# The last two experts' outputs added by one-hot products in PSUM

## What is computed

```python
combine = jnp.sum(jax.nn.one_hot(expert_id, N_EXPERTS) * (g_w[:, None] * top_w)[..., None], axis=1)
def expert_step(acc, inp):
    wg, wu, wd, c = inp
    hid = jax.nn.silu(t @ wg) * (t @ wu)
    return acc + c[:, None] * (hid @ wd), None
y, _ = lax.scan(expert_step, jnp.zeros_like(t), (w_gate, w_up, w_down, combine.T))
x = x + y
return rmsnorm(x, final_norm_w)
```

## Time and profile before

| | |
|---|---|
| time before, median of 3 runs | 468.01 us (467.56 to 470.87) |
| span of the profiled execution | 468.6 us, 7159 instructions |
| PE, PEld, DVE busy | 447.5, 387.4, 343.1 us (96%, 83%, 73%) |
| ACT, POOL busy | 275.6, 159.2 us (59%, 34%) |
| DMA | 94.57 MB, mean 202 GB/s |
| chain that ended last | PE 60%, DVE 20%, DMA 9%, ACT 6% |

### The profile page before, as it was taken

The page is one execution under the profiler, slowest core; times in us unless marked ns, Lnnn a source line. Parts: engine busy times, 40 slices in busy tenths (PEclk is TensorE's granted clock), DMA queues, the critical chain, the costliest instruction groups (busy, mean ns, idle before and its releaser), DMA issues.

```text
span 468.6 us, 7159 instructions
## 1 busy us (share of the span) xinstructions
PE 447.5 (96%) x2769; PEld 387.4 (83%) x2769; DVE 343.1 (73%) x527; ACT 275.6 (59%) x462; POOL 159.2 (34%) x120
## 2 busy tenths in 40 slices
PE   8999999999999899999999998999999999999873
PEld 7678887899997798999999988888888888888641
DVE  4456999756768889899775358677887788777835
ACT  6753555235562162338253335689999999979525
POOL 4660000000004001113300404288878887885210
PEclk9999999999999999999999998999999999999979
DMA  8850223240202033143299512989999999998256
GB/s 306 342 234 25 88 90 111 78 166 8 91 0 92 15 121 121 61 147 124 84 374 306 234 39 61 321 306 368 380 374 350 374 376 380 364 328 326 95 180 237
DMA packets 21200, 94.57 MB, mean 202 GB/s; under 512 B 4860, under 2 KB 7080, under 8 KB 12840
## 3 DMA queue, kind: packets, MB, share of 16 engines
q1 hardware_dynamic: 14424, 83.53, 47.7%
q0 software_dynamic: 4096, 8.41, 5.5%
q10 hardware_dynamic: 2640, 2.11, 1.4%
HBM read 88.79 MB, written 11.54 MB: 214 GB/s over the span
## 4 chain that ended last, share of the span: by engine, by line
PE 60%; DVE 20%; DMA 9%; ACT 6%; issue 3%; SPq 0%; DVEq 0%; POOLq 0%; ACTq 0%
PE bank L1695 32%; DMA raw<-in_w_gate_up_dram 5%; PE bank L2031 5%; PE bank L2033 5%; PE bank L2032 4%; DVE arena L1186 3%; PE bank L2019 2%; PE bank L1771 2%; DVE wl L1107 2%; PE bank L1896 2%; DMA arena<-pairs_dram 1%; ACT wh L765 1%; DMA pairs_dram<-arena 1%; DVE actl L1566 1%; DMA X<-h_dram,arena 1%
## 5 line engine op out<-in xcount | busy, mean ns | idle before, releaser
L1695 PE MATMUL bank<-wh,acth 128*128 128x256 f32 x320 | 91.9, 287 | 0.8 <-DVE actl L1101 0.8
L1695 PE MATMUL bank<-wh,actl 128*128 128x256 f32 x320 | 90.6, 283 | 0.0
L1695 PE MATMUL bank<-wl,acth 128*128 128x256 f32 x320 | 90.6, 283 | 0.0
L1695 PEld LDWEIGHTS bank<-wh,acth 128*128 128x128 f32 x320 | 61.3, 192 | 1.1 <-issue 1.0
L630 POOL TENSOR_TENSOR wl<-raw,wh 128x2048 fp32r<-128x2048 f32 x4 | 20.2, 5038 | 122.0 <-ACT wh L765 122.0
L1695 PEld LDWEIGHTS bank<-wl,acth 128*128 128x128 f32 x320 | 61.3, 192 | 0.0
L1695 PEld LDWEIGHTS bank<-wh,actl 128*128 128x128 f32 x320 | 61.3, 191 | 0.0
L709 POOL TENSOR_TENSOR wl<-raw,wh 128x1024 fp32r<-128x1024 f32 x15 | 36.0, 2417 | 42.7 <-ACT wh L960 42.7
L2031 PE MATMUL bank<-wh,acth 128*128 128x512 f32 x124 | 50.0, 403 | 0.1
L2033 PE MATMUL bank<-wh,actl 128*128 128x512 f32 x124 | 48.7, 393 | 0.0
L2032 PE MATMUL bank<-wl,acth 128*128 128x512 f32 x124 | 48.4, 390 | 0.0
(11 more groups left out here) (378 smaller groups left out, 1038.6 us busy)
## 6 DMA issues: line engine op xcount, KB each, us to landing
arena<-in_w_gate_up_dram SPq DMA_DIRECT2D x18, 1024.0 KB, 15.1
raw<-in_w_units_dram SPq DMA_DIRECT2D x17, 1024.0 KB, 4.9
arena<-in_w_down_dram SPq DMA_DIRECT2D x16, 1024.0 KB, 13.2
raw<-in_w_gate_up_dram SPq DMA_DIRECT2D x14, 1024.0 KB, 15.6
arena<-pairs_dram SPq DMA_DIRECT2D x6, 512.0 KB, 7.2
arena<-in_x_first_dram SPq DMA_DIRECT2D x3, 768.0 KB, 7.8
arena<-in_x_dram SPq DMA_DIRECT2D x4, 512.0 KB, 12.5
arena<-in_x_dram SPq DMA_DIRECT2D x1, 2048.0 KB, 11.0
```

The costliest lines, as they stand in the source:

```text
L1695: ins = te.matmul(acc_ap, a, b, start=(j == 0), stop=(j == n - 1))
```

## The change

A new list LAST names the last two experts in the order, 14 and 15. Their outputs are no longer scattered to memory and loaded back.

- Early in the run, SP copies x to the 512 late rows of pairs_dram (memory to memory), so that rows which no expert has written hold finite values; POOL and DVE wait for that copy (xrows_in).
- gates moves from the end of the loop to just behind expert 1 on DVE, with four more small instructions there, and four (slot_rows) that bring the token number of each slot of experts 14 and 15 into a tile. SP stores the late gates to gates_dram at expert 8, POOL gathers them by slot with two small indirect DMAs at expert 12 (slot_gates), and sets two small tiles to zero earlier.
- For experts 14 and 15, DVE writes chosen[j], a 112 x 512 one-hot from slot to token (choose). PE writes their down products to banks 2, 3 and 7, 4, without waiting for the copies of the expert before. ACT's copy into ysb multiplies by the gate of the slot.
- SP loads the late rows when experts 0 to 13 are scattered, not 0 to 15. Early tiles 0 and 1 get their gate and residual on POOL (multiplication of tile 0, both additions) and ACT (multiplication of tile 1, behind a wait for all four early loads, in ACT's program of expert 14, ahead of the copy of expert 15's hidden activation; the square root table is loaded there too). Tiles 2 and 3 stay on DVE.
- DVE writes late * r1[19] + early into PSUM, two halves of 128x512 for each of the 4 tiles (base_ok). The factor r1[19] is the late gate, or 0 where the token's late expert is 14 or 15. PE then adds two products per half, chosen[j] with ysb, onto it: 16 f32 products of 128x512. All four tiles are squared by ACT and scaled by DVE out of PSUM, as tiles 2 and 3 were.
- The products L2120, L2123 and L2128 go. The branch to later rounds stands at the end of every engine's program (all_rounds; for SP ahead of the stores), with a second set of sums inside it.

```diff
-        late_diag = [gate[:, 0, i * P:(i + 1) * P] for i in range(2)]
+        LAST = (NE - 2, NE - 1)
+        chosen = [raw[:, 0, j * T:(j + 1) * T] for j in range(2)]
+        slot_gate = [part(4) for _ in LAST]
+        slot_row = part(2 * TT).rearrange("p (j t) -> p j t", j=2)
...
-        def later_rounds(eng, body):
+        last_cols = slice(PERM[LAST[0]], PERM[LAST[1]] + 1, PERM[LAST[1]] - PERM[LAST[0]])
+        out_banks = {LAST[0]: (2, 3), LAST[1]: (7, 4)}
+        sum_banks = ((0, 1), (5, 6), (2, 3), (7, 4))
+        FIN = TT + 1
+
+        def down_banks(e, first_round):
+            return out_banks.get(e, (5, 6)) if first_round else (5, 6)
+
+        def all_rounds(eng, body, before=None, after=None):
 
             eng.wait_ge(routed, 1)
             n = eng.value_load(rounds[0:1, 0:1], min_val=1, max_val=MOST)
             with eng.If(n > 1):
-                with eng.Fori(1, n) as r:
+                eng.wait_ge(fin_ok, FIN)
+                if before is not None:
+                    before()
+                with eng.Fori(1, n + 1) as r:
                     body(r, r * NE)
-            return n
+                if after is not None:
+                    after(n)
 
...
+                if u == U["i"][0]:
+                    sp.dma_start(pairs_dram[T:2 * T, :], x[0]).then_inc(xrows_in, 16)
             sp.wait_ge(hg_ev, TT)
-            sp.dma_start(xres, x[0].rearrange("(t p) n -> p t n", p=P)).then_inc(xres_in, 16)
+            sp.dma_start(xres, x[0].rearrange("(t p) n -> p t n", p=P)).then_inc(xrows_in, 16)
...
-                        if e == 0:
-                            sp.wait_ge(early_ok, r * TT)
-                        else:
-                            sp.wait_ge(wlb_ok, (base + max(e - WSETS + 1, 0)) * 2)
+                        sp.wait_ge(wlb_ok, (base + max(e - WSETS + 1, 0)) * 2)
                         load_b(e)
-
-            def load_early(rows_done, first_round=False):
+                    if first_round and e == NE // 2:
+                        sp.wait_ge(gates_ok, 1)
+                        sp.dma_start(gates_dram.rearrange("(t p) n -> p t n", p=P), rs).then_inc(small_dma, 16)
+
+            def scattered(rows_done):
                 for j in range(YB):
                     sp.wait_ge(sca_out[j], rows_done)
-                if first_round:
-                    wait_a(sp, 0, NE - 2)
-                    sp.wait_ge(wlb_ok, (NE - 2) * 2)
+
+            def load_early():
                 for tt in range(TT):
                     sp.dma_start(early[tt], pairs_dram[tt * P:(tt + 1) * P, :]).then_inc(early_in, 16)
 
-            def sp_later(r, base):
-                sp_round(r, base)
-                load_early(r * (16 * PER_Y) + 16 * PER_Y)
+            def load_late():
+                for tt in range(TT):
+                    sp.dma_start(late[tt], pairs_dram[T + tt * P:T + (tt + 1) * P, :]).then_inc(row_in[tt], 16)
+
...
-            load_early((NE - G) // YB * 16, True)
-            n = later_rounds(sp, sp_later)
-            for j in range(YB):
-                sp.wait_ge(sca_out[j], n * (16 * PER_Y))
-            for tt in range(TT):
-                sp.dma_start(late[tt], pairs_dram[T + tt * P:T + (tt + 1) * P, :]).then_inc(row_in[tt], 16)
+            scattered((NE - G) // YB * 16)
+            wait_a(sp, 0, NE - 2)
+            sp.wait_ge(wlb_ok, (NE - 2) * 2)
+            load_early()
+            sp.wait_ge(xrows_in, 32)
+            scattered((NE - len(LAST)) // YB * 16)
+            load_late()
+            all_rounds(sp, sp_round, after=sp_sums)
...
+            def slot_gates(j, e):
+                pool.wait_ge(small_dma, 48)
...
-                    scatter(r, base, e)
+                    if first_round and e == NE - HGB:
+                        for j, last in enumerate(LAST):
+                            slot_gates(j, last)
+                    if not (first_round and e in LAST):
...
-            later_rounds(pool, pool_round)
+            pool.wait_ge(gates_ok, 1)
+            pool.wait_ge(early_in, 16 * TT)
+            ch.link(gp.tensor_tensor(early[0], early[0], r1[:, 10, 0:1].broadcast_to([P, D]), ALU.mult))
+            pool.wait_ge(early_ok, 1)
+            for tt in range(2):
+                gp.tensor_tensor(early[tt], early[tt], xres[:, tt, :], ALU.add).then_inc(early_ok, 1)
...
-                elif e + 1 < NE:
+                elif e + 1 < NE and not first_round:
                     round_hidden(step + 1, e + 1)
+                if first_round and e == LAST[0]:
+                    act.wait_ge(early_in, 16 * TT)
+                    act.wait_ge(gates_ok, 1)
+                    sc.activation(early[1], early[1], ACT.Copy, scale=r1[:, 10, 1:2]).then_inc(early_ok, 1)
+                    ch.link(sc.activation(dec[:, 0, 0:1], ident[:, 0:1], ACT.Sqrt))
+                    round_hidden(step + 1, e + 1)
+                low, high = down_banks(e, first_round)
                 act.wait_ge(dn, step * 2 + 3)
                 y_free(act, r, e, first_round)
-                sc.activation(ysb[e % YB][:, 0:512], bank[5][:, :], ACT.Copy).then_inc(y0_ok, 1)
+                if first_round and e in LAST:
+                    act.wait_ge(gates_dma, 16 * len(LAST))
+                    weight = slot_gate[LAST.index(e)][0:CAP, 1:2]
+                    sc.activation(ysb[e % YB][0:CAP, 0:512], bank[low][0:CAP, :], ACT.Copy,
+                                  scale=weight).then_inc(y0_ok, 1)
+                    act.wait_ge(dn, step * 2 + 4)
+                    sc.activation(ysb[e % YB][0:CAP, 512:1024], bank[high][0:CAP, :], ACT.Copy,
+                                  scale=weight).then_inc(y1_ok, 1)
+                    return
...
-            n = later_rounds(act, act_round)
-            act.wait_ge(early_ok, n * TT)
-            for i in range(2):
-                sc.activation(late_diag[i], ident[:, :], ACT.Copy, scale=r1[:, 11, 2 + i:3 + i]).then_inc(diag_in, 1)
-            ch.link(sc.activation(dec[:, 0, 0:1], ident[:, 0:1], ACT.Sqrt))
-            for tt in range(2):
...
+                if first_round and e in LAST:
+                    choose(LAST.index(e))
...
-                if first_round:
-                    gates()
-                dve.wait_ge(early_in, r * (16 * TT) + 16 * TT)
+                    if first_round and e == 1:
+                        slot_rows()
+                        gates()
+
+            def choose(j):
+                wait_a(dve, 0, NE - HGB + 1)
+                ve.tensor_tensor(chosen[j].rearrange("p (t s) -> p t s", t=TT),
+                                 iota1.unsqueeze(1).broadcast_to([P, TT, P]),
+                                 slot_row[:, j].unsqueeze(2).broadcast_to([P, TT, P]),
+                                 ALU.is_equal).then_inc(chosen_ok, 1)
+
+            def slot_rows():
                 for tt in range(TT):
-                    ve.scalar_tensor_tensor(early[tt], early[tt], r1[:, 10, tt:tt + 1], xres[:, tt, :], ALU.mult,
-                                            ALU.add).then_inc(early_ok, 1)
+                    ve.tensor_scalar(slot_row[:, :, tt], gix[:, last_cols], float(1 - tt * P), None, ALU.add)
...
+                ve.tensor_tensor(r1[:, 19], mb[:, :, PERM[LAST[0]]], mb[:, :, PERM[LAST[1]]], ALU.add)
...
+                dve.wait_ge(h2_st, 16 * (n_front - n_in + 1))
+                ve.tensor_copy(rs[:, :, 1], r1[:, 11])
+                ch.link(ve.tensor_tensor(r1[:, 0], r1[:, 11], r1[:, 19], ALU.mult))
+                ve.tensor_tensor(r1[:, 19], r1[:, 11], r1[:, 0], ALU.subtract).then_inc(gates_ok, 1)
...
+            dve.wait_ge(early_in, 16 * TT)
+            ch.link(add_early(2))
+            for tt in range(TT):
+                dve.wait_ge(row_in[tt], 32)
+                if tt < 2:
+                    dve.wait_ge(early_ok, tt + 2)
+                if tt == 1:
+                    dve.wait_ge(y1_ok, NE - 1)
+                elif tt == 2:
+                    dve.wait_ge(y1_ok, NE)
+                elif tt == 3:
+                    dve.wait_ge(y1_ok, NE + 1)
+                for h in range(2):
+                    c = slice(h * 512, (h + 1) * 512)
+                    ve.scalar_tensor_tensor(bank[sum_banks[tt][h]][:, :], late[tt][:, c], r1[:, 19, tt:tt + 1],
+                                            early[tt][:, c], ALU.mult, ALU.add).then_inc(base_ok, 1)
+                if tt == 1:
+                    ch.link(add_early(3))
...
+            def dve_sums(n):
...
+                if first_round and e == LAST[1]:
+                    pe.wait_ge(six_ok, 1)
                 for h in range(2):
-                    pe.wait_ge(y0_ok if h == 0 else y1_ok, step + 1)
+                    if not (first_round and e in LAST):
+                        pe.wait_ge(y0_ok if h == 0 else y1_ok, step + 1)
...
-            pe_round(0, 0)
-            n = later_rounds(pe, pe_round)
-            pe.wait_ge(early_ok, n * TT)
-            for tt in range(2, TT):
```

(23 more changed lines are left out.)

112 lines of the change are left out of this document (67 added, 45 removed).

## The result

Five executions of each kernel, taken side by side: 474.60 us after (473.64 to 475.16) against 468.01 us before (467.56 to 471.04), ratio 1.0117 with the 95% interval 1.0086 to 1.0147. The change costs 1.2%, some 5.5 us by this ratio; the two medians lie 6.6 us apart. The profiled execution of after took 475.16 us and has a span of 473.0; before's profiled span was 468.6.

The account below looks back on a forecast made before the run. PE, busy 96%, does the same expert products; the 23.3 us behind the last expert output decide. Steps gave span 466.7, earlier parts 0.4 (467.1), clock 1.7 (468.8); less the 0.6 offset, 468.2 us, range 463.0 to 473.0.

Parts of the forecast that it names:

- Earlier parts: Gates behind expert 1 add 3.1 us on DVE; PE slips 1.2, transfers take most up; 0.4 taken.
- POOL beside DVE: POOL's early additions beside two-input DVE instructions: contention could make the sum 0.6 higher; taken as 0.
- Step 1: In expert 14 ACT waits for the early loads until 440.6; expert 15's hidden copy moves to 443.2, +2.7 us.
- The clock: PE idles 2.2 us before the last down products; the clock then falls, costing 1.7 us (or 0 or 3.3).
- step 2: PE has expert 15's operands at 444.1; down products end 3.3 us later, at 447.3, last copy at 448.0.
- Steps 2 and 3: Down products end at 447.3; PSUM bases by POOL and DVE, first half written from 446.8, are hidden behind PE.
- Step 4: 16 f32 sums on PE at 0.86 each take 13.7 us at full clock; the last begins at 460.2.
- The rival that put the sums at the low level: PE's final sums run at the low clock level: measured 469.8, or 480 for all 16; chance 0.15.
- Step 5: Behind the last sum: 1.14 to ACT's square, then 5.3 to the end; span 466.7.
- The branch rival: DVE's jump over later rounds, behind its last scaling, ends the span 1.4 later: measured 468 to 469.6; chance 0.18.
- The offset: Span to time: before's profiled span 468.6 is 0.6 above its 468.0 median, so 468.8 becomes 468.2 us.
- Late rows: SP loads them once expert 13's scatter lands, 6.9 after issue; rival: lands at 10.7, measured 469.8, chance 0.05.

Follow-up runs that it names:

- gates_gap: The changed kernel with gates and slot rows moved ahead of expert 0's second token pass, where DVE waits and POOL is idle: 472.67 us, ratio 1.0101.
- act_free: The changed kernel without ACT's wait for the early loads; DVE does all four early tiles, POOL none: 469.70 us, ratio 0.9986.
- warm: The changed kernel with 14 unread products on PE in the gap before expert 15's down products: 473.70 us, ratio 1.0109.
- no_branch: act_free_gap with the branch to further rounds left out on every engine, so only the first round is computed: 467.12 us, ratio 0.9977.
- act_free_gap: act_free with the gates placed as in gates_gap: 468.19 us, ratio 1.0006.
- pool_off: The changed kernel with POOL's three early operations given to DVE, ACT's wait and scaling kept: 472.11 us, ratio 1.0061.
- pool_off_warm: pool_off with 14 unread products in PE's gap before the last down products: 472.03 us, ratio 1.0054.

## Why the prediction was wrong, by its steps

The forecast was 468.2 us in a range of 463.0 to 473.0; measured were 474.6. In the profiles the span is 4.2 us above the forecast's 468.8: 3.4 of them stand before the first sum (452.84 against the 449.4 of its terms), 0.8 behind.

- **Earlier parts**, the step that failed first. "PE slips 1.2 ... set by the transfers and not by PE, which takes most of it up; I take 0.4 of bounds 0 and 1.2." It was 2.54 at expert 2, above the upper bound, and still 1.87 at the last turn. Two errors. The duration of DVE's pair was taken as fixed when it was moved by 2.5 us; but it moved onto POOL's pair, and grew from 2.36 to 4.54 (POOL's from 4.78 to 6.81). At the slack of 1.9 a delay of 2.5 alone would have cost PE 0.6. gates_gap shows it: same gates, no meeting, 2.2 of the 2.54 us gone. And the DMA in the chain was read as a limit of the transfers. The weights of the last expert landed as much later as PE was. Before, they landed at 430.3; ACT's rounding of them after, in the timeline:

```profile
432.57 2.01 ACT L1014 ACTIVATE wh<-raw 128x1024 fp32r<-128x1024 f32 x2 [0.38 <-DMA raw<-in_w_gate_up_dram]
```

  Its issue moved from 408.1 to 410.7, with the slip: the load had been released by the engines' own pace, and absorbed nothing.
- **POOL beside DVE**, the term taken as 0. The rows chosen were POOL's, and POOL's additions were indeed not slower: 1.89 and 5.14, 7.0 against the 7.3 worked out. DVE's instructions were, by 0.85 and 2.12. The Trainium skill, GPSIMD Engine Reference, Key points, says that GpSimd shares its SBUF interfaces with VectorE and contends when VectorE's instruction has two SBUF inputs or runs in a 2-port mode; the traces agree on who meets, and put the price on either side, 2.2 us of a 2.36 us pair. I applied the rule to POOL alone and only at the end, and chose the row that made it nothing.
- **Step 1, ACT's wait.** Right in mechanism and place: the wait is in the forecast's order, and act_free, without it, has the first sum 5.6 us sooner behind the turn. Its size was low: the copy stood at 446.33 and not 443.2. The early rows landed at 443.6 instead of 440.6, since they were issued 3.3 later (430.1 against 426.8), 2.54 of it the slip of expert 2, and took 13.46 as against 13.8. The slip and the wait were added as if independent, but the wait ends with a transfer that the slip delays.
- **The clock.** The gap came (3.45 us, 443.78 to 447.23) and the clock fell to 1.2 GHz for the rest of the down products, 2.6 us lost (5.5 instead of 2.9; the 3.3 of step 2 hold 0.4 in which PE was still busy with expert 14) against the 1.7 taken. But warm shows that this is not a term of a sum: the late bases stood behind it.
- **Steps 2 and 3.** With a first sum at 452.84 the bases (first half done at 452.7) and the output were ready together, so "these are hidden" was true by a hair in the profiled execution and false in warm.
- **Step 4** held: 0.86 a product, 14.1 for all. The rival that put the sums at the low level did not occur; the clock was back at 1.00 when they began.
- **Step 5 and the branch.** From ACT's last square to the end 6.0 us against 5.3. The branch rival, given 0.18 as an alternative, happened besides, and no_branch prices it at 0.9 in the span and 0.3 outside it, but in the landing of the stores and not in a jump behind the last scaling.
- **The offset.** "The profiled span of 468.6 is 0.6 above the median of 468.0, so the same offset." Time and span of one execution lie 1.75 apart for the kernel before (1.75 or 1.76 as the median of each of the four sessions). By that distance a span of 468.6 belongs to an execution of about 470.4, 2.3 above the median, and the median execution has a span of about 466.3. Taken so, even the forecast's own span of 468.8 meant 470.9 us, with the 2.1 that after's executions lie above theirs.
- **Late rows.** The scatter of expert 13 landed 7.0 behind its issue and the late loads were not waited for: this step was right, and its rival did not occur.

By the ratios, after lies 1.17% above before, some 5.5 us. The gates' place and ACT's wait with what hangs on it make 1.11% of it (after to act_free_gap, 5.2 us), the branch 0.29% (act_free_gap to no_branch, 1.4 us), and what the change gives without them is -0.23% (no_branch, -1.1 us, interval -2.0 to -0.1). The division of the first part is read from the profiles: the last turn stands 1.9 us later than before, and the way from it to the end falls by 5.8 us when ACT's wait goes. The expected gain was there, and small: in the profiles the way from the last turn to the end is 28.5 us before and 24.8 in no_branch, while the sixteen fp32 sums alone take 14 us.

What stays open: the clock's own share in what ACT's wait cost. Filling the gap gave nothing that could be told from none, with POOL and without, but the landing of the early rows changed between executions by 2.7 us (440.96 in warm, 443.64 in the changed kernel), as much as the clock could cost.

## What to carry to other kernels

When you move work on DVE, ask what POOL runs at the moment where the displaced DVE instructions will land: check the timelines of both engines, and look for a place where POOL is idle, not one where DVE has slack. Do not set a wait for a transfer on the engine that feeds the last products; give the early work to an engine that is idle there, and put a branch ahead of the last stores if it can be. And before a span is turned into a time, take the pair of one and the same execution.

## What the hardware showed that was not expected

- DVE with two SBUF operands and POOL's tensor_tensor take nearly the sum of their times when they meet: both pairs are done after 6.81 us, where 2.36 and 4.78 make 7.14. DVE's is done after 4.54; alike in five kernels (the changed one, act_free, warm, pool_off, pool_off_warm). Who pays differs: at the end DVE paid most (3.40 instead of 1.28) and POOL little if anything (5.14 for two additions; no run has them alone, and its two subtractions alone take 4.78).
- Four DVE operations of two columns took 4.30 us beside POOL's pair instead of 0.38, one of them 2.39, and one of four columns took 2.02: size is no protection. DVE instructions with an operand in PSUM were not held: in the changed kernel the low part of the hidden activation takes 0.41 at 327.63, inside POOL's 6.81.
- Behind PE's idle time of 3.45 us the granted clock, 1.00 until 446, was 0.50 from 447 to 453; in pool_off, where PE was idle for 0.97 us at that place, it stayed at 1.00.
- The branch past the further rounds, as the last thing on each engine, costs 0.9 us in the span and 0.3 beyond it; the output's stores take up to 4.2 us to land instead of 2.6.
